# Who asks for the value pages of the decode: the sync engine alone, or Pool and the sync engine in turn

## The reference, cut to what matters

```python
pk = cache_k[page_table].reshape(DB, P, H_A, 2, DK_A)      # DB = 8, P = 16 pages x 128 tokens
pv = cache_v[page_table].reshape(DB, P, H_A, DV_A)
s = jnp.einsum('bqhmd,bkhmd->bhmqk', q, k) * (DK_A ** -0.5)
p = jax.nn.softmax(jnp.where(mask, s, -jnp.inf), axis=-1)
w = p[:, :, 0] - lam * p[:, :, 1]
return jnp.einsum('bhqk,bkhd->bqhd', w, v)
```

## Time and profile before

| | us |
|---|---|
| median of three runs | 992.28 |
| lowest and highest | 991.8 and 998.51 |
| the profiled execution, its own time | 997.07 |
| span of its profile | 995.4 |
| TensorE busy | 930.8 |
| mean granted TensorE clock over the span | 0.983 |
| value requests by Pool | 72 of 256 KB, 4.8 us to landing (median) |
| value requests by the sync engine | 56 of 256 KB, 4.0 us to landing (median) |

### The profile page before, as it was taken

The page is one execution under the profiler, slowest core; times in us unless marked ns, Lnnn a source line. Parts: engine busy times, 40 slices in busy tenths (PEclk is TensorE's granted clock), DMA queues, the critical chain, the costliest instruction groups (busy, mean ns, idle before and its releaser), DMA issues.

```text
span 995.4 us, 18461 instructions
## 1 busy us (share of the span) xinstructions
PE 930.8 (94%) x6963; PEld 749.5 (75%) x6963; DVE 490.2 (49%) x1079; ACT 389.4 (39%) x832; POOL 108.6 (11%) x233
## 2 busy tenths in 40 slices
PE   3999989999999999998799999998869999999996
PEld 3999989999888888887566667765547786577774
DVE  4634844555474345444475655455464443533222
ACT  5533253433334643333544544454453222421211
POOL 1300000000000000002000023331011000000000
PEclk9989999999999999999999999999999999999998
DMA  6362215222332222223977779967984422203221
GB/s 216 105 172 65 65 50 142 65 64 65 101 106 65 85 64 66 82 65 117 344 247 216 233 256 337 345 220 239 313 283 176 180 85 69 64 18 131 74 90 42
DMA packets 115265, 142.36 MB, mean 143 GB/s; under 512 B 9623, under 2 KB 75799, under 8 KB 115178
## 3 DMA queue, kind: packets, MB, share of 16 engines
q1 hardware_dynamic: 109418, 122.31, 38.4%
q0 software_dynamic: 5760, 18.88, 5.6%
HBM read 125.34 MB, written 15.41 MB: 141 GB/s over the span
## 4 chain that ended last, share of the span: by engine, by line
PE 83%; ACT 4%; DMA 4%; DVE 3%; SPq 3%; issue 2%; POOL 1%; POOLq 0%; ACTq 0%; DVEq 0%
PE ps L1944 72%; PE ps L1947 10%; DMA Vr<-in_cache_v 1%; SPq L579 1%; DMA Kr<-in_cache_k 1%; DMA xrow<-in_x_prompt 1%; PE ps L1939 1%; ACT U L922 1%; SPq L575 1%; DVE pp L1758 0%; ACT wh L938 0%; ACT junk L1214 0%; ACT pp L1136 0%; POOL small L734 0%; DVE kTs L1723 0%
## 5 line engine op out<-in xcount | busy, mean ns | idle before, releaser
L1944 PE MATMUL ps<-hhi,whi 128*128 128x272 f32 (+1 forms) x672 | 229.1, 341 | 1.1 <-DVE hlo L1279 1.1
L1944 PE MATMUL ps<-hhi,wlo 128*128 128x272 f32 (+1 forms) x672 | 219.8, 327 | 0.0
L1944 PE MATMUL ps<-hlo,whi 128*128 128x272 f32 (+1 forms) x672 | 219.2, 326 | 0.0
L1944 PE MATMUL ps<-wh,r 128*128 128x512 f32 (+1 forms) x544 | 154.8, 401 | 0.1
L1944 PEld LDWEIGHTS ps<-hhi,whi 128*128 128x128 f32 x672 | 129.5, 193 | 13.8 <-issue 3.7
L1944 PEld LDWEIGHTS ps<-hlo,whi 128*128 128x128 f32 x672 | 129.5, 193 | 9.9 <-issue 1.9
L1944 PEld LDWEIGHTS ps<-hhi,wlo 128*128 128x128 f32 x672 | 129.2, 192 | 9.2
L1944 PEld LDWEIGHTS ps<-wh,r 128*128 128x128 f32 (+1 forms) x544 | 99.1, 185 | 26.1 <-issue 1.0
L1295 DVE TENSOR_TENSOR wlo<-wst,whi 128x1024 fp32r<-128x1024 f32 x56 | 69.2, 1236 | 80.4 <-ACT whi L897 80.4
L1723 DVE COPY kTs<-ps 128x512 f32<-128x512 f32 x64 | 44.1, 689 | 66.6 <-PE ps L1947 66.5
L1947 PEld LDWEIGHTS ps<-ident,Kr 128*128 128x128 f32 x512 | 56.3, 141 | 25.5 <-issue 22.0
(11 more groups left out here) (351 smaller groups left out, 1372.0 us busy)
## 6 DMA issues: line engine op xcount, KB each, us to landing
Kr<-in_cache_k SPq DMA_DIRECT2D x128, 256.0 KB, 4.2
wst<-in_w_in SPq DMA_DIRECT2D x56, 512.0 KB, 3.9
Vr<-in_cache_v POOLq DMA_DIRECT2D x72, 256.0 KB, 4.8
Vr<-in_cache_v SPq DMA_DIRECT2D x56, 256.0 KB, 4.0
out_y_prompt<-rows SPq DMA_DIRECT2D x16, 512.0 KB, 2.9
xrow<-in_x_prompt SPq DMA_DIRECT2D x8, 512.0 KB, 5.1
wout<-in_w_out SPq DMA_DIRECT2D x8, 512.0 KB, 5.5
rows<-in_x_prompt SPq DMA_DIRECT2D x8, 512.0 KB, 4.4
```

What stands on the lines that cost most here:

```text
L1944: return nc.tensor.matmul(out, lhsT, rhs, start=start, stop=stop, **more)
```

## The change

The value steps from 36 on are shared: the even ones are asked for by Pool, the odd ones by the sync engine, each where it stood in the order of positions. The sync engine loads its list of eight pages ahead of the first odd step of a group of four. Pool loads its list ahead of the first even one, as it did for 0 to 35. The semaphores follow: TensorE waits for an odd step from 37 on at the semaphores of the sync engine, for all others at those of Pool. The number of transfers, their sizes and their places in `Vr` stay.

```diff
--- before.py
+++ after.py
@@ -104,7 +104,7 @@
 VALUES_AT = {n: m for m, n in enumerate(VALUE_STEP)}
 TURNS_AT = {n: [bt for bt in TURNS if TURN_STEP[bt] == n] for n in range(STEPS_OF_DECODE)}
 FIRST_VALUES = [20 + 3 * q for q in range(4)]
-VALUES_BY_SP = 36
+SHARED_FROM = 36
 PHASES = 4
 ATTEND = CH * [0.95]
 for u in range(UNITS + 4):
@@ -149,6 +149,11 @@
 OT.insert(OWN, XT[CH])
 GATED = [OWN] + [j for j in range(9) if j != OWN]
 QUARTER = D // 4
+
+
+def values_by_sp(q):
+
+    return q >= SHARED_FROM and q % 2 == 1
 
 
 def early(i):
@@ -571,9 +576,9 @@
             value_page = [None] * GROUPS
 
             def value_pages(q):
-                if q % 4 == 0:
+                if q % 4 == 1:
                     value_page[:] = nc.values_load_multi_w_load_instructions(
-                        ptab[0:1, q * GP:q * GP + GROUPS], engines=[mybir.EngineType.SP], min_val=0, max_val=POOL - 1)[1]
+                        ptab[0:1, (q - 1) * GP:(q - 1) * GP + GROUPS], engines=[mybir.EngineType.SP], min_val=0, max_val=POOL - 1)[1]
                 sp.wait_ge(s["v_used"], q - 3)
                 for k in range(GP):
                     sp.dma_start(Vr[:, GP * (q % 4) + k, :],
@@ -592,8 +597,9 @@
                 for n in range(DECODED[pos - 1] if pos else 0, DECODED[pos]):
                     if n + 4 < KEY_STEPS:
                         key_pages(n + 4)
-                    if VALUES_BY_SP <= VALUES_AT.get(n - 1, 0) + 4 < KEY_STEPS:
-                        value_pages(VALUES_AT[n - 1] + 4)
+                    q = VALUES_AT.get(n - 1, KEY_STEPS) + 4
+                    if q < KEY_STEPS and values_by_sp(q):
+                        value_pages(q)
                 turn_at = pos - CH
                 if turn_at == 0:
                     sp.wait_ge(*done["krow_stored"])
@@ -856,7 +862,7 @@
                     heads_root(u // H - 1)
                 for n in range(DECODED[pos - 1] if pos else 0, DECODED[pos]):
                     q = FIRST_VALUES.index(n) if n in FIRST_VALUES else VALUES_AT.get(n - 1, KEY_STEPS) + 4
-                    if q < VALUES_BY_SP:
+                    if q < KEY_STEPS and not values_by_sp(q):
                         value_pages(q)
                     if n == MERGE_STEP:
                         root(ss4[:, 0:1], rs4[:, 0:1], done["as_norm"], 11 + CH, "as_hrs")
@@ -2256,10 +2262,10 @@
 
             def values(m):
                 b, v, j = key_step(m)
-                if m < VALUES_BY_SP:
+                if values_by_sp(m):
+                    pe.wait_ge(late_v_in[m % 4], 32 * ((m - SHARED_FROM) // 4 + 1))
+                else:
                     pe.wait_ge(v_in[m % 4], 32 * (m // 4 + 1))
-                else:
-                    pe.wait_ge(late_v_in[m % 4], 32 * ((m - VALUES_BY_SP) // 4 + 1))
                 if m % IN_BATCH == 0:
                     pe.wait_ge(s["pT_act"], turned(b, NEW))
                     pe.wait_ge(*done["vrow_stored"])
```

## The result

The changed kernel takes 998.25 us (median of 20 runs, 993.83 to 1003.23), the kernel before 994.11 us (20 runs, 991.27 to 998.51). The ratio is 1.0031, with a 95% interval of 1.0017 to 1.0044: 3.1 us slower (1.7 to 4.4). The forecast was 1.25 us less, and a median inside 986 to 997.

The account below looks back on a forecast made before the run. TensorE was taken as the bound, busy 930.8 of 995.4 us. The terms -4.4 + 1.3 - 1.85 + 1.3 + 1.5 + 0.5 + 0.4 gave -1.25 us, from a median of 992.28 to 991.0 us; 8-in-10 range 986 to 997.

Parts of the forecast that it names:

- (7): Behind the stall the low clock can return: +0.4 us, between 0 and 1.7; Pool's 536 ns requests are covered.
- (1): Steps 40 to 42: 2.7 us of waits and 1.7 us lost to the low clock behind them go: -4.4 us.
- (2): Transfers at 688 to 694 us must follow; idle capacity is worth 3.1 us, so new waits come back: +1.3 us.
- (3): Steps 46 to 53: half of 3.7 us of waits goes through earlier requests: -1.85 us, between nothing and 3.7.
- (4): Requests queue behind Pool's roots: a 4.5 us stall at step 56, net +1.3 (+0.5 to +2.8); step 48 +1.5 us.
- (5): Step 36's request stands ahead of the fourth group's root, delaying TensorE's turn behind it: +0.5 us, bounds 0 and 1.3.
- (6): Steps 61 to 63: 1.0 us of waits go, but the turn at 740.08 would be late next: 0.
- The third rival: Engines that move data are the bound, each removed wait comes back later: 0, 992.3 us; chance 0.10.
- The second rival: Slower: Pool's roots hold the pages at 48 and 56 at upper prices: +4.8 us, 997.1 us; chance 0.17.

Follow-up runs that it names:

- Dose (9): The kernel before with 28 more tiny transfers asked for by Pool at about 475 us, value steps unmoved: ratio 1.0021 to the kernel before.
- 10: The kernel before with one more DRAIN on Pool at about 755 us: ratio 0.9999 to the kernel before.
- 11: The changed kernel with one more DRAIN on Pool at about 755 us: ratio 1.0015 to the kernel before.
- experiments 2: The changed kernel with Pool's root of head group 5 put behind the request for step 56: ratio 1.0011 to the kernel before.
- 3: The changed kernel, but from step 38 Pool loads its page list behind the previous group's request, ahead of the roots: ratio 1.0001 to the kernel before.
- 4: The kernel before with step 56 alone asked for by Pool, behind its root of group 5: ratio 1.0015 to the kernel before.
- the first: The changed kernel run again with no edit: ratio 1.0033 to the kernel before.
- experiment 8: The changed kernel with step 56 alone given back to the sync engine: ratio 1.0038 to the kernel before.
- 12: The changed kernel with Pool's root of group 5 behind the request for step 56 and a DRAIN at about 755 us: ratio 1.0010.
- 15: A repeat of the changed kernel with root of group 5 behind the request for step 56 and the mid-program DRAIN: ratio 0.9988.
- 13: The changed kernel with root of group 5 behind step 56's request, three wout requests moved to units 29 to 31, and the mid-program DRAIN: 0.9974.
- 17: A repeat of the changed kernel with root behind step 56's request, late wout requests and the mid-program DRAIN: ratio 0.9976, 992.79 us.

## Why the prediction was wrong, by its own steps

**The cost that the sum did not have.** Step (7) put a Pool request at 536 ns against 333 and called it covered. It costs 536 ns there, and is covered there, but it is charged a second time at the program's end, 82 ns each in Pool's DRAIN. In the trace of before this row stood at 6.57 us and ended 0.5 us behind the sync engine's last row: its cover was already gone, and 28 requests more go straight to the time, 2.3 us. The prediction read no row behind 745 us. Dose (9) shows it in the rows and in the time: 2.3 us in the profile, 2.1 us (0.2 to 4.0) in the runs. Removal (10, 11) shows it in the rows, and its times agree without being clear of noise. This is 2.3 of the 3.1 us.

The steps of the sum follow. Where I give means, they are over the five profiles of the kernel before (with 9 and 10) and the four of the changed one (with 11), from TensorE's rows.

**(1) and (2), 2.7 us at steps 40 to 42 and 1.7 us of low clock, less 1.3 us: half right.** The DMA share of that work rose from 0.46 to 0.77 and the wait at 40 is gone in each of the four profiles, but 41 to 45 now take 1.4 to 3.4 us (2.4 in the first profile). The waits of 40 to 45 fell from 3.4 to 2.6 us on the mean: 0.9 us gained in place of 1.4. The low clock behind 694 us was no fixed term: of five profiles of the kernel before and its variants three have it (3.4, 6.8 and 6.8 us), two don't. The changed kernel has none there, in four profiles. By the mean of 3.4 us of low clock some 1.7 us of work are gained, an estimate, as taken.

**(3), half of the 3.7 us at 46 to 53: too large.** In the first profile 1.7 us remain, as forecast. On the means, without step 48, the waits fell from 3.0 to 1.7 us: 1.3 us in place of 1.85.

**(4), the stall at 56: right in its mechanism, a little small in size.** Forecast 4.5 us, measured 4.9, 5.6, 5.1 and 4.6 us. Its place, its cause (the root ahead of the request, then the list) and its replacement of the waits at 56 and 57 hold; experiments 2 and 3 shorten it, and 4 brings it about with one step. On the means it is 5.1 us where 56 and 57 waited 2.9: +2.2 in place of +1.3, inside its bounds. At 48 I expected 1.5 us; in three of four profiles nothing came, in one 1.05 us. That the waits ahead of it gave Pool the time is likely and not shown.

**(5), the root of group 3: right.** The idle time ahead of that turn is 2.2 us in all four profiles where it is 1.55 in all five: +0.7 for +0.5.

**(6): right in its sum alone.** The waits of 61 to 63 were to go and the turn behind them to be late in their place. They did not go: the first profile waits 1.0 us at 62, as much as before at 62 and 63.

**(7), the clock behind the stall: too small.** 0.4 us was taken; the clock stood at 0.50 for 6.8 us in each of the four profiles, beginning while TensorE still stood. In the first TensorE was busy for 3.95 of the 6.8 us, which at half the clock is some 2.0 us of work, an estimate (1.7 to 2.7 us in the others, by the same working). In the kernel before two of five have a low clock there (3.4 and 6.8 us), 1.0 us of work on the mean. So the change adds some 1.3 us where 0.4 stood, and takes back most of what (1) gained by the clock.

Together: -1.25 us was forecast for the value stretch. Four profiles of the changed kernel average 61.8 us, five of the kernel before (two of them its variants) 61.7. So it is level, with 1 us of scatter in each group, which leaves about 1.6 us to either side: a gain of 1.25 us in the stretch is not excluded, and not seen. Taken straight, the bounds of (3), (4), (5) and (7) add up to 987.5 to 996.5 us and not to 994.5 as the prediction has it. The third rival, no change, describes the stretch best. Its rule of the Trainium skill (DMA: Bandwidth & Descriptors, "Issuing engines are not separate DMA queues"), that DMAs started from several engines run on the same 16 and save only the issuing sequencer's time, agrees with this: 61.8 us against 61.7. By the steps above, the longer stall at 56 and its low clock took back what was gained at 40 to 53; that is a reading of the profiles' means and no experiment by itself. The second rival had the right sign and the wrong place: it put the loss into the stretch. That it came near the measured number is luck.

One thing behind the stretch speaks for the change. From the end of step 63 to the last matmul the changed kernel takes 244.7 to 245.2 us in four profiles, the kernel before 245.3 to 246.2 us in five, 0.8 us more on the mean. A low clock begins within 6 us of the end of the stretch in all nine; it lasts 6.8 us in each of the four, and 6.8 to 13.7 us in the five. Whether the one makes the other was not tested.

**What stays open.** 3.1 less 2.3 leaves 0.8 us, with an interval from -0.6 to +2.1 us, so that nothing is shown about it; the 0.8 us gained behind the stretch make what is to be explained larger. What the stall at 56 is worth in time is not settled: experiments 2 and 3 gave 2.2 and 3.2 us back against the first, experiment 8 took the stall away and gave nothing, and 12 and 15 differ by 2.2 us for one kernel. Of the gain of 13 and 17 the DRAIN explains 0.5 us against the kernel before; root, wout and the sharing were not separated for the rest.

## What to carry to other kernels

A request that is moved to another engine has to be costed to the end of the program: look at the closing rows of every engine, which one ends last, and whether its duration counts something that the change adds to. Two single profiles can differ by 4 us before the changed code has begun; compare a stretch with fixed first and last instructions, and have more than one profile of each kernel before a difference of 2 us is believed. Where a helper engine takes over requests, put them ahead of its waits for others where the order allows: here that cut the wait at step 56 from 5.6 to 2.3 us.

## What the runs showed of the hardware that I had not expected

Pool's DRAIN at the end takes 0.65 us where no DMA request of Pool precedes it since the last DRAIN, and 82 ns more for each request: 6.57 us at 72, 6.74 at 74, 8.70 at 98, 8.86 at 100, independent of the size (16 bytes or 2 KB to a partition). A DRAIN in the middle of the program takes 7.0 us at 72 and 9.3 us at 100, after which the last one takes 0.65 us; where Pool is idle it cost nothing that the times show (0.9999, 0.9984 to 1.0014). The DRAINs of the other engines at the end take 0.01 to 6 us and do not change between the kernels. The sync engine's takes 7 ns, though it asks for 348 to 376 DMAs.
